# Two groups of heads in one step: the local attention of a two-block layer stack

## The reference

```python
def sliding_window_attention(q, k, v, sinks):        # BLOCK = WINDOW = 128, 2 groups of 4 heads, head width 64
    qb = q.reshape(b, nb, BLOCK, N_KV_HEADS, GQA_GROUP, HEAD_DIM)
    kk, vv = with_prev(k), with_prev(v)              # own block and the one before: 256 keys
    scores = jnp.einsum('bnqhgd,bnkhd->bnhgqk', qb, kk) * scale
    scores = jnp.where(valid, scores, -jnp.inf)
    m = jnp.maximum(jnp.max(scores, axis=-1, keepdims=True), sink)
    p = jnp.exp(scores - m)
    denom = jnp.sum(p, axis=-1, keepdims=True) + jnp.exp(sink - m)
    out = jnp.einsum('bnhgqk,bnkhd->bnqhgd', p / denom, vv)
...
y_conv = (cb * causal_dwconv_2(cc * cx, conv_mix_w)) @ w_conv_out
y_attn = sliding_window_attention(q, k, v, sinks) @ w_attn_out + b_attn_out
merged = sigmoid(g_conv) * y_conv + sigmoid(g_attn) * y_attn
```

## Time and profile before

| | |
|---|---|
| median of 3 runs | 1676.45 us (1676.13 to 1678.28) |
| the profiled execution | 1675.05 us, span 1673.3 us |
| TensorE, matmuls | 97% busy, 7828 instructions |
| VectorE | 53% busy |
| ScalarE | 36% busy |
| GpSimd | 10% busy |

### The profile page before, as it was taken

The page is one execution under the profiler, slowest core; times in us unless marked ns, Lnnn a source line. Parts: engine busy times, 40 slices in busy tenths (PEclk is TensorE's granted clock), DMA queues, the critical chain, the costliest instruction groups (busy, mean ns, idle before and its releaser), DMA issues.

```text
span 1673.3 us, 19688 instructions
## 1 busy us (share of the span) xinstructions
PE 1619.5 (97%) x7828; PEld 1342.0 (80%) x7828; DVE 893.5 (53%) x1239; ACT 598.0 (36%) x866; POOL 172.0 (10%) x138
## 2 busy tenths in 40 slices
PE   6899999989999999999999999999999999999996
PEld 5689898988778888888887777777788888888885
DVE  4676754645335534343656666644555564564554
ACT  4533323433324414232443333354333332332231
POOL 4141221202002000000034100000002000000000
PEclk9899999999999999999999999999999999999998
DMA  7111111353113232333222222221232233223221
GB/s 249 41 38 51 42 48 51 102 168 102 58 38 114 88 101 88 102 100 108 88 88 89 76 89 76 76 89 63 77 122 96 87 101 109 88 90 114 89 76 51
DMA packets 42843, 147.32 MB, mean 88 GB/s; under 512 B 4800, under 2 KB 4928, under 8 KB 42624
## 3 DMA queue, kind: packets, MB, share of 16 engines
q1 hardware_dynamic: 40608, 140.68, 25.4%
q10 hardware_dynamic: 1584, 2.88, 0.5%
q0 software_dynamic: 560, 2.50, 0.4%
HBM read 143.94 MB, written 2.10 MB: 87 GB/s over the span
## 4 chain that ended last, share of the span: by engine, by line
PE 63%; issue 24%; DVE 6%; ACT 3%; POOL 2%; DMA 1%; ACTq 0%; SPq 0%; POOLq 0%; DVEq 0%
PE bank L1124 18%; PE bank L1125 18%; PE bank L1126 18%; DVE temp L1631 1%; POOL square_sum L2041 1%; PE bank L1254 1%; PE bank L1236 1%; PE bank L1317 1%; PE bank L1334 1%; DMA x_first<-x_in 1%; PE bank L1259 1%; PE bank L1374 1%; DVE w_lo L1638 1%; PE bank L1083 1%; PE bank L1354 1%
## 5 line engine op out<-in xcount | busy, mean ns | idle before, releaser
L1124 PE MATMUL bank<-a_hi,w_hi 128*128 128x512 f32 (+1 forms) x1368 | 534.3, 391 | 13.2 <-DVE a_lo L1646 13.1
L1125 PE MATMUL bank<-a_lo,w_hi 128*128 128x512 f32 (+1 forms) x1368 | 523.3, 383 | 0.0
L1126 PE MATMUL bank<-a_hi,w_lo 128*128 128x512 f32 (+1 forms) x1368 | 523.2, 382 | 0.0
L1638 DVE TENSOR_TENSOR w_lo<-w_raw,w_hi 128x1024 fp32r<-128x1024 f32 (+2 forms) x267 | 344.5, 1291 | 195.3 <-ACT w_hi L1391 194.6
L1391 ACT ACTIVATE w_hi<-w_raw 128x1024 fp32r<-128x1024 f32 (+2 forms) x267 | 274.8, 1031 | 196.0 <-PE bank L1126 195.9
L1124 PEld LDWEIGHTS bank<-a_hi,w_hi 128*128 128x128 f32 x1368 | 260.0, 190 | 67.7 <-issue 15.4
L1126 PEld LDWEIGHTS bank<-a_hi,w_lo 128*128 128x128 f32 x1368 | 260.1, 190 | 50.2
L1125 PEld LDWEIGHTS bank<-a_lo,w_hi 128*128 128x128 f32 x1368 | 260.1, 190 | 47.7 <-issue 1.2
L1124 PE MATMUL bank<-b_hi,w_hi 128*128 128x512 f32 x720 | 281.4, 391 | 0.4 <-ACT b_hi L1521 0.4
L1125 PE MATMUL bank<-b_lo,w_hi 128*128 128x512 f32 x720 | 280.2, 389 | 0.0
L1126 PE MATMUL bank<-b_hi,w_lo 128*128 128x512 f32 x720 | 280.2, 389 | 0.0
(11 more groups left out here) (268 smaller groups left out, 1201.5 us busy)
## 6 DMA issues: line engine op xcount, KB each, us to landing
w_raw<-weights_in SPq DMA_DIRECT2D x251, 512.0 KB, 3.3
w_raw<-weights_in SPq DMA_DIRECT2D x8, 384.0 KB, 3.0
xs<-x_in ACTq DMA_DIRECT2D x8, 256.0 KB, 5.6
w_raw<-weights_in SPq DMA_DIRECT2D x8, 256.0 KB, 2.6
out<-xs SPq DMA_DIRECT2D x8, 256.0 KB, 2.2
x_first<-x_in SPq DMA_DIRECT2D x6, 256.0 KB, 11.9
mem_x<-mem_in POOLq DMA_DIRECT2D x1, 1024.0 KB, 12.7
matrices<-matrices_in POOLq DMA_DIRECT2D x1, 640.0 KB, 8.8
```

Source lines behind the costliest of these rows:

```text
L1124: pe.matmul(to, w_hi[:, slot, at], hi, start=k == k0, stop=False)
L1125: pe.matmul(to, w_hi[:, slot, at], lo, start=False, stop=False)
L1126: t = pe.matmul(to, w_lo[:, slot, at], hi, start=False, stop=k == k1 - 1)
L1638: dve.tensor_tensor(w_lo[:, n % SLOTS, 0:size], raw[:, n % SLOTS, 0:size], w_hi[:, n % SLOTS, 0:size].bitcast(F32), ALU.subtract).then_inc ...
```

## The change

Attention's pairs are ordered block, pair, group, and the two groups are handled in one step. The scores of both groups are one visit of TensorE: the matmuls of group 0 (partitions 0 to 63) and group 1 (64 to 127) alternate, into two banks. Both turns are one visit. The values of both groups are one visit in each block, alternating, into partitions 0 to 63 and 64 to 127 of one bank, and one copy of 128x512 takes them out. `scores2` and `soft2` have four buffers, `probs2_t` two. The scores pair and the turn pair are steps of their own: 21 steps instead of 25.

```diff
-PAIRS = [(n, g, pair) for n in range(NC) for g in range(KVH) for pair in range(QT // 2)]
+PAIRS = [(n, g, pair) for n in range(NC) for pair in range(QT // 2) for g in range(KVH)]
+PER_BLOCK = KVH * QT // 2
...
     def window_attention():
-        add("scores", 0)
+        for g in range(KVH):
+            add("scores", g)
         yield
-        for count, (n, g, pair) in enumerate(PAIRS):
-            if count + 1 < len(PAIRS):
-                add("scores", count + 1)
-            add("turn_probs", count)
+        for count in range(0, len(PAIRS), KVH):
+            for g in range(KVH):
+                if count + KVH + g < len(PAIRS):
+                    add("scores", count + KVH + g)
             yield
-            if pair == QT // 2 - 1:
-                add("attended", n * KVH + g)
+            for g in range(KVH):
+                add("turn_probs", count + g)
+            yield
+            if (count + KVH) % PER_BLOCK == 0:
+                add("attended", count // PER_BLOCK)
                 yield
...
-    interleave(conv_branch(), window_attention(), 5 * KT, NC * KVH * 3 + 1)
+    interleave(conv_branch(), window_attention(), 5 * KT, NC * (2 * QT // 2 + 1) + 1)
...
-                elif kind == "scores":
+                elif kind == "scores" and n % KVH == 0:
...
                     for i in range(2):
-                        t = pe.matmul(b[:, i, :], q2[part, 2 * pair + i, chunk(block)], k2[part, (block + 1) * P - width:(block + 1) * P],
-                                      start=True, stop=True)
-                    t.then_inc(scores_pe.handle, 1)
+                        for count in range(n, n + KVH):
+                            block, g, pair, halves, width, part = window(count)
+                            b = side("scores", count)[:, 0:2 * width].rearrange("p (h k) -> p h k", h=2)
+                            t = pe.matmul(b[:, i, :], q2[part, 2 * pair + i, chunk(block)], k2[part, (block + 1) * P - width:(block + 1) * P],
+                                          start=True, stop=True)
+                            if i == 1:
+                                t.then_inc(scores_pe.handle, 1)
...
                     for a in range(halves):
-                        t = pe.matmul(bank[part, :], v2[:, block - halves + 1 + a, part],
-                                      probs2_t[:, a, :, :].rearrange("p h q -> p (h q)"), start=a == 0, stop=a == halves - 1)
+                        for g in range(KVH):
+                            part = slice(g * HD, (g + 1) * HD)
+                            t = pe.matmul(bank[part, :], v2[:, n - halves + 1 + a, part], probs2_t[g][:, a, :, :].rearrange("p h q -> p (h q)"),
+                                          start=a == 0, stop=a == halves - 1)
...
-                    dve.tensor_copy(q2[part, :, chunk(block)], side("attended", n)[part, :].rearrange("p (h q) -> p h q", h=QT)
-                                    ).then_inc(attended_dve.handle, 1)
+                    dve.tensor_copy(q2[:, :, chunk(n)], side("attended", n).rearrange("p (h q) -> p h q", h=QT)).then_inc(attended_dve.handle, 1)
```

More of the change, by code:

```diff
@@ L644, in side_turns @@
     if kind in ("row", "rates", "decays", "mix_bias", "sums", "mix", "decay", "turn", "out", "mem_v_turn", "rotate",
-                "value", "scores", "turn_probs", "attended"):
+                "value", "turn_probs", "attended"):
         return one((kind, n))
+    if kind == "scores":
+        return all_at_once(*((kind, n + g) for g in range(KVH))) if n % KVH == 0 else []
     if kind == "scales":
@@ L785, in build_program @@
         merged = sbuf("merged", [P, KT, S], stack=second)
[L786 to L788 removed]
+        scores2 = [sbuf(f"scores2_{i}", [P, 2 * 2 * P], stack=second) for i in range(2 * KVH)]
+        probs2_t = [sbuf(f"probs2_t{i}", [P, 2, QT, P], stack=second) for i in range(KVH)]
+        soft2 = [sbuf(f"soft2_{i}", [P, 5, 2], stack=second) for i in range(2 * KVH)]
         second.close()
@@ L994, in b_source @@
             if g == B_ATTN:
[L995 removed]
+                return q2[:, n, :], attended_dve.at(NC - 1)
             if g == B_MERGED:
@@ L1347, in tensor_program @@
                     t.then_inc(value_pe.handle, 1)
-                elif kind == "scores":
-                    block, g, pair, halves, width, part = window(n)
-                    b = side("scores", n)[:, 0:2 * width].rearrange("p (h k) -> p h k", h=2)
+                elif kind == "scores" and n % KVH == 0:
                     q.wait_ge(*rotate_pool.at(QT))
-                    wait_side("scores", n)
+                    for g in range(KVH):
+                        wait_side("scores", n + g)
                     for i in range(2):
-                        t = pe.matmul(b[:, i, :], q2[part, 2 * pair + i, chunk(block)], k2[part, (block + 1) * P - width:(block + 1) * P],
-                                      start=True, stop=True)
-                    t.then_inc(scores_pe.handle, 1)
+                        for count in range(n, n + KVH):
[5 more added lines that the diff above has]
+                                t.then_inc(scores_pe.handle, 1)
                 elif kind == "turn_probs":
                     block, g, pair, halves, width, part = window(n)
-                    s = scores2[n % 2][:, 0:2 * width].rearrange("p (h k) -> p h k", h=2)
+                    s = scores2[n % (2 * KVH)][:, 0:2 * width].rearrange("p (h k) -> p h k", h=2)
                     b = side("turn_probs", n)[:, 0:2 * width].rearrange("p (a h q) -> p a h q", a=halves, h=2)
@@ L1367, in tensor_program @@
                 elif kind == "attended":
-                    block, g, pair, halves, width, part = window(n * QT // 2)
+                    halves = window(n * PER_BLOCK)[3]
                     bank = side("attended", n)
-                    q.wait_ge(*turn_probs_act.at(n * (QT // 2) + QT // 2 - 1))
+                    q.wait_ge(*turn_probs_act.at((n + 1) * PER_BLOCK - 1))
                     q.wait_ge(*value_act.at(0, 2))
@@ L1568, in scalar_program @@
                     block, g, pair, halves, width, part = window(n)
-                    s = scores2[n % 2][:, 0:2 * width].rearrange("p (h k) -> p h k", h=2)
-                    biggest, bias, total, sink, inverse = (soft2[n % 2][:, i, :] for i in range(5))
+                    s = scores2[n % (2 * KVH)][:, 0:2 * width].rearrange("p (h k) -> p h k", h=2)
+                    biggest, bias, total, sink, inverse = (soft2[n % (2 * KVH)][:, i, :] for i in range(5))
                     q.wait_ge(*scores_dve.at(n, 4))
```

22 lines of the change are left out of this document (11 added, 11 removed).

## The result

The changed kernel takes 1656.05 us in the median of 4 runs (1653.38 to 1660.4), the kernel before, on the same chip, 1676.29 (1675.69 to 1678.28): a ratio of 0.9887, 95% interval 0.9873 to 0.9901. The profiled execution took 1655.96 us with a span of 1654.1; against the 1675.05 and 1673.3 of before that is 19.1 and 19.2 us.

A forecast was written before the change was run, and what follows sets the result against it. TensorE, busy 97% of the span, was taken as the bound. Fewer visits 4.3, two waits 1.9 and overlapping halves 6.9 summed to 13.1 us saved, from 1676.45 to 1663.3 us; range 1660.3 to 1671.5.

The forecast's parts named there:

- 12 visits fewer: TensorE in the attention: 8 scores visits instead of 16, 4 values visits instead of 8, each 0.36 us; saves 4.3 us.
- two waits gone: TensorE's waits for turned probabilities (1.0 us) and scaled scores (0.9 us) disappear in the new step order; saves 1.9 us.
- both halves at once: Scores and values matmuls of the two groups overlap on TensorE's halves; saves 6.9 us, range 5.6 to 8.7.
- price per change of half: TensorE's 34 changes of half inside scores and values visits: taken as 0, possible 0 to 12.2 us.
- wait at block 1's values: Tightest values visit: copies done at 18.1, wanted at 18.5 or 19.2 us; costed at nothing, under 1 us if late.
- behind the stretch: After the attention's stretch no change was expected; a span change outside 937 to 1190 us would show the prediction wrong.
- the upper bound of the overlap: Most that overlapping halves could save in scores and values visits: 8.1 us, or 8.7 with narrow scores.
- The rival that would have made the kernel slower: Each of 34 changes of half costs up to 0.36 us: 6.0 us slower, 1682.5 us; chance 0.09 for any price.
- nothing overlaps: Scores and values gain nothing from two halves; only visits and waits save, 6.2 us, 1670.2 us; chance 0.16.
- one kind overlaps only: Only scores overlap (10.0 us saved, 1666.4) or only values (10.4 us, 1666.0); chance 0.20, half each.
- VectorE's queue otherwise: Weight splits behind a scores pair are held up 6.9 instead of 3.4 us on VectorE, still hidden by 5.6 us.
- the copy out: Eight copies of 64x512 become four of 128x512 at 0.69 us: 2.7 us off VectorE, not on the path.

The follow-up runs named there:

- the run of 0, 0, 1, 1: Changed kernel with both matmuls of group 0 issued before both of group 1 inside each visit, instead of alternating; 1657.07 us, ratio 0.9897.
- the third experiment: Changed kernel with each group's scores as a step of its own, 16 scores visits instead of 8, turns and values still paired; 1666.21 us, ratio 0.9955.
- the four in one: Changed kernel with a block's four scores in one visit, 4 visits instead of 8, values a step later; 1654.01 us, ratio 0.9883.
- The kernel with more on VectorE: Changed kernel with eight tiny memsets added on VectorE, off the path; one run, 1655.97 us.

## Why the prediction was wrong

The direction was right, and so was the mechanism as far as both kinds of matmul overlap; the size of the overlap was wrong, because of a stagger between the halves that isn't there, and two small terms were missing.

| term | predicted | measured |
|---|---|---|
| 12 visits fewer | 4.3 | 3.7 |
| two waits gone | 1.9 | 2.05 |
| both halves at once | 6.9 (5.6 to 8.7) | 12.0 |
| price per change of half | 0 | 0 |
| wait at block 1's values | 0 (cover 0.4 to 1.1) | -0.45 |
| behind the stretch | 0 | 1.5 |
| sum | 13.1 | 18.8 of 19.2 in the spans |

**The step that failed** is the upper bound of the overlap: "a matmul's two records use one half and must follow each other; the second may run beside the first of the other half. Eight records then take five slots, not eight." The first clause holds. The second lets the halves run only staggered by a record, as if a single line fed both. The trace shows them starting 6 to 7 ns apart, all four records of each side by side: eight records in four slots. From the rows: six wide scores visits x 4 x 0.213 = 5.1; three values visits x 4 x 0.427 = 5.1; block 0, two slots of values and two visits of narrow scores, 0.85 each. That is 11.9, against the 12.0 measured by moving both groups to one half. The narrow scores, taken as bound by their loads and costed at 0, double too. No row stood behind that stagger: a load under a running matmul of its own half says only that loads aren't in the way, and from there the sum should have gone to four slots as its upper end; with 4.3 + 1.9 + 12.0 that end would have been 18.2 us saved. So the bound, more than the choice inside it, kept the result out of the range. Not the bound alone: with 18.2 and the same 1.2 for scatter the range would have begun at 1657.1, and 1656.05 is still 1.0 below; the 1.5 us behind the stretch are more than that.

The Trainium skill (TensorE: Matmul & The Clock Gate, The mechanism, in its Part 3) has matmuls on different tiles start some 4 ns apart; here it is 6 to 7 ns, or 13 with two matmuls of the other half ahead, so the nearly equal start agrees, though not the figure. Its strict order of matmuls does not agree with the run of 0, 0, 1, 1, where group 1's first matmul starts ahead of group 0's second. Nor does its statement that loads overlap only where the row group differs agree with the values: their halves share all 128 rows, and four records on each take 1.94 us, as four alone did. The measurement decides in both.

**Right: no price for a change of half.** A visit that changes halves costs 1.27 us, and one that doesn't, the single group of the third experiment, 1.27. The rival that would have made the kernel slower is refuted, and so are "nothing overlaps" and "one kind overlaps only": scores and values each double.

**Nearly right: the visits.** The 0.36 us is a whole coming and going. The spread scores and the four in one measure 0.42 and 0.40 for a visit that stands alone; joining two kinds saves 0.21, half of it. Before, 15 of 16 scores visits left into a turn, and a wide one cost 1.20 there, where one alone costs 1.27; in the new order that cheaper exit is gone, hence 3.7 instead of 4.3.

**Right: the two waits; missed: a new one.** The values of block 1, all engines in order of time, changed kernel:

```profile
1032.00 0.39 PE L1133 MATMUL bank<-a_hi,w_lo 128*128 128x512 f32 x1
...
1032.63 1.22 DVE L1650 TENSOR_TENSOR w_lo<-w_raw,w_hi 128x1024 fp32r<-128x1024 f32 x1
1033.77 0.68 DVE L1636 TENSOR_TENSOR temp<-bank,rstd 128x512 f32<-128x512 f32 x1
...
1047.27 0.68 DVE L1636 TENSOR_TENSOR temp<-bank,rstd 128x512 f32<-128x512 f32 x1
...
1049.53 0.73 ACT L1602 ACTIVATE temp<-temp,columns 128x512 f32<-128x512 f32 x1 [0.82 <-DVE temp L1980]
1050.16 1.06 ACT L1595 ACTIVATE probs_t<-bank 128x512 f32<-128x512 f32 x2
1051.27 1.94 PE L1386 MATMUL bank<-probs_t,v 128*64 128x512 f32 x8 [0.39 <-ACT probs_t L1595]
```

TensorE's last matmul of cb5 ends at 1032.39. The prediction had the values wanted 18.5 us after that, and they were (1051.27 less the idle 0.39 is 1050.88). It had the two copies done at 18.1; they are done at 18.8 (1051.22). The difference stands at the front of the queue: a weight split, 1032.63 to 1033.85, is ahead of the cb chain on VectorE, so the chain starts 1.4 us after the matmul and not 0.2. The chain of engines was right, a cover of 0.4 us was too thin for one forgotten entry, and its price was under 1 us, as stated. Moving the values a step later took the wait away.

**Right: VectorE's queue otherwise, table loads, the copy out.** No weight split is among TensorE's waits.

**Not foreseen: 1.5 us behind the last projection matmul.** The prediction named a change outside 937 to 1190 us as a sign of being wrong, and this is one. The stretches from there to the end, before:

```profile
1656.30:1673.30 17.00, 4.29 (x18) 3.56 (x16) 6.90 (x11) 0.63 (x1) 1.01 (x1) 0.57 0.33 124
```

and after:

```profile
1638.50:1654.10 15.60, 4.05 (x18) 3.27 (x16) 6.90 (x11) 0.63 (x1) 1.01 (x1) 0.59 0.36 134
```

The same instructions. 0.3 us are eight records of the small matmuls that sum the squares, 1.87 us before and 1.57 after. They ran at a mean granted clock of 0.50 before and 0.62 after, and in the second traces of the two kernels they took 1.67 and 1.05 us, so this part varies from one execution to the next. 1.1 us are the last store, which lands 3.3 instead of 2.25 us after its issue. In both traces of the kernel before, one packet of instructions lies among these stores:

```profile
q14 instruction: 1, 0.01, 0.1%
```

In none of the eleven traces of the changed kernel and its variants is there one among the stores, and in none is the store late. That is an association. The kernel with more on VectorE had a packet, but ahead of the stores, so what places that packet stays open. The rest of the 20.2 us of the medians, about 1 us, is within the scatter of the runs.

## What to carry to other kernels

When two matmuls use different halves of the array, take as the upper bound that the second costs nothing at all, and as the lower that nothing overlaps; a bound built from an imagined way of issuing is no bound. Interleave the halves matmul by matmul, since the look past a busy half is short (three waiting records here), and gather the half-width work into few visits, at 0.4 us each, as long as no visit needs a bank or an operand that another engine has just been given. Where a cover comes out under half a microsecond, list every entry that the queue holds between its two ends, the splits of other tiles too, or plan a step more.

## What was not expected of the hardware

- Two fp32 matmuls on the two halves run at twice the pace in either form: different rows (scores) or the same rows and different columns (values), and with 128 columns as with 256 or 512. Wide scores visits took 1.27 us against 2.13 on one half, narrow ones 0.85 against 1.29, values 2.07 against 3.78.
- TensorE starts the other half's record past three waiting ones (13 ns behind the first), not past four; in the latter case a visit of eight and eight records took 3.10 us instead of 2.14, four and a half slots more.
- After TensorE had stood for 3.3 us, and for 1.9 us too, it went on at a granted clock of 0.50; with waits of 0.4 us, and of 1.0 us in the kernel before, the clock stayed at 1.00.
